# MLA prompt attention: the chunk mask as an extra matmul of one row, instead of a 97th row of queries and keys

## The reference, cut to what matters

```python
def _chunk_mask(q_pos, k_pos):
    return (k_pos // CHUNK)[None, :] <= (q_pos // CHUNK)[:, None]      # CHUNK = 64

def core(qb, qp):                                                      # qb: 128 queries
    s = jnp.einsum('bqhd,bkhd->bhqk', qb, k).astype(jnp.float32) * scale
    p = _masked_softmax(s, _chunk_mask(qp, kpos))
    return jnp.einsum('bhqk,bkhd->bqhd', p.astype(v.dtype), v)
```

## Time and profile before

| what | before |
|---|---|
| median of 3 runs | 4433.84 us (4428.59 to 4433.85) |
| the profiled execution | 4433.85 us |
| span of its trace | 4432.1 us |
| mean granted TensorE clock | 0.904 |
| MATMUL busy | 3834.7 us, 87% of the span |
| LDWEIGHTS busy | 3452.6 us, 78% |
| VectorE busy | 1939.3 us, 44% |
| ScalarE busy | 1147.2 us, 26% |
| GpSimd busy | 834.1 us, 19% |
| expanding stage, layers 0 and 1 | 704.5 to 716.3 us and 2870.6 to 2882.3 us |
| attention stage, layers 0 and 1 | 716.3 to 822 us and 2882.3 to 2988 us |

### The profile page before, as it was taken

How to read it: one execution, slowest core, us unless ns; L and a number is a source line. 1 busy time by engine, 2 the same in 40 slices (tenths; PEclk the granted TensorE clock), 3 DMA queues, 4 the chain that set the end, 5 groups by cost and what they waited for, 6 DMA issues and landing times. The chain is left out here.

```text
span 4432.1 us, 52290 instructions
## 1 busy us (share of the span) xinstructions
PE 3834.7 (87%) x21498; PEld 3452.6 (78%) x21498; DVE 1939.3 (44%) x3099; ACT 1147.2 (26%) x2101; POOL 834.1 (19%) x694
## 2 busy tenths in 40 slices
PE   3887798889779999999878769887988799999996
PEld 2865587579679999999866657864978799999995
DVE  3355243255334444454444634333542444444454
ACT  2244113333122221212133421242321321221211
POOL 1211011011122232222122100200112222232220
PEclk8999599789789999999989977995988899999998
DMA  4511121010101111111062210111001011111111
GB/s 150 165 59 55 44 70 70 22 48 1 31 27 39 43 43 39 39 39 43 19 181 92 72 61 30 61 57 67 1 6 44 28 39 39 43 39 38 44 39 47
DMA packets 102912, 229.80 MB, mean 52 GB/s; under 512 B 29156, under 2 KB 64484, under 8 KB 99016
## 3 DMA queue, kind: packets, MB, share of 16 engines
q1 hardware_dynamic: 102664, 226.36, 16.0%
HBM read 171.90 MB, written 52.07 MB: 51 GB/s over the span
## 5 line engine op out<-in xcount | busy, mean ns | idle before, releaser
L244 PE MATMUL PS<-h_split,w_split 128*128 128x384 f32 x3072 | 1069.1, 348 | 100.9 <-PEq L183 100.9
L246 PE MATMUL PS<-h_split,w_split 128*128 128x384 f32 x3072 | 1051.8, 342 | 0.0
L245 PE MATMUL PS<-h_split,w_split 128*128 128x384 f32 x3072 | 1048.6, 341 | 0.0
L239 POOL TENSOR_TENSOR w_split<-w_full,w_split 128x1024 fp32r<-128x1024 f32 (+1 forms) x196 | 494.4, 2523 | 1371.6 <-ACT w_split L231 1369.5
L244 PEld LDWEIGHTS PS<-h_split,w_split 128*128 128x128 f32 x3072 | 594.9, 194 | 116.7 <-issue 114.6
L245 PEld LDWEIGHTS PS<-h_split,w_split 128*128 128x128 f32 x3072 | 588.1, 191 | 1.4 <-issue 0.3
L246 PEld LDWEIGHTS PS<-h_split,w_split 128*128 128x128 f32 x3072 | 587.5, 191 | 0.0
L231 ACT CAST w_split<-w_full 128x1024 fp32r<-128x1024 f32 (+1 forms) x196 | 204.6, 1055 | 905.7 <-PE PS L246 763.5
L244 PE MATMUL PS<-ffn_act,w_split 128*128 128x384 f32 x1056 | 368.7, 349 | 71.8 <-DVE x L2035 54.5
L2035 DVE TENSOR_TENSOR x<-x,PS 128x384 f32<-128x384 f32 x528 | 287.1, 553 | 239.7 <-PE PS L246 239.5
L245 PE MATMUL PS<-ffn_act,w_split 128*128 128x384 f32 x1056 | 367.3, 348 | 0.0
(11 more groups left out here) (339 smaller groups left out, 5910.5 us busy)
## 6 DMA issues: line engine op xcount, KB each, us to landing
w_full<-in_w_up SPq DMA_DIRECT2D x88, 512.0 KB, 3.5
w_full<-in_w_down SPq DMA_DIRECT2D x44, 512.0 KB, 3.5
w_full<-in_w_in SPq DMA_DIRECT2D x40, 512.0 KB, 3.7
kq_keep<-split_rows SPq DMA_DIRECT2D x128, 128.0 KB, 2.4
kq_row<-kq_keep SPq DMA_DIRECT2D x32, 512.0 KB, 4.2
x_keep<-x SPq DMA_DIRECT2D x2, 4608.0 KB, 19.3
x<-x_keep SPq DMA_DIRECT2D x2, 4608.0 KB, 14.4
w_full<-in_w_out SPq DMA_DIRECT2D x16, 512.0 KB, 3.5
```

The source lines that it names most:

```text
L239: pool.tensor_tensor(ws[:, n % SSLOTS, 1, 0:w], wf[:, n % WSLOTS, 0:w], ws[:, n % SSLOTS, 0, 0:w].bitcast(F32), ALU.subtract).then_inc(w_l ...
L244: pe.matmul(out, w_hi, a_hi, start=first, stop=False)
L245: pe.matmul(out, w_hi, a_lo, start=False, stop=False)
L246: return pe.matmul(out, w_lo, a_hi, start=False, stop=last)
```

## The change

The mask no longer rides on a 97th row. GpSimd's four writes of row 96 are gone, and `qT` is declared with 96 rows. In `scores` the last 128 keys are no longer a matmul of their own, but part of the last piece of at most 512 keys; after it a matmul with one row, `first_half` (1 for the first 64 queries) times `second_half` (-1e30 for the last 64 keys), adds the mask to the last 128 columns in PSUM. Both operands are constants that already lie in row 0 of `cst8`. `prompt_attention` is called once, with `comps` 1 and `bias` None, so `masked` is true for the last piece of every unit.

```diff
-        qT = at("qT", [97, HEADS, TOK], R(30))
+        qT = at("qT", [96, HEADS, TOK], R(30))
...
                     for hh in range(HEADS):
                         pool.tensor_copy(kT[64:96, hh, :], krT[64:96, 0:SEQ])
-                    for half in range(2):
-                        cols = slice(64 * half, 64 * half + 64)
-                        pool.memset(qT[96:97, :, 0:SEQ].rearrange("p h (i c) -> p h i c", c=P)[:, :, :, cols],
-                                    1.0 - half)
-                        pool.memset(kT[96:97, :, :].rearrange("p h (i c) -> p h i c", c=P)[:, :, :, cols],
-                                    NEG * half)
...
-                    for at in range(0, n - P, 512):
-                        w = min(512, n - P - at)
-                        pe.matmul(S(v, 0)[:, at:at + w], q_of(hh, i, 96), k_of(hh, at, w, 96), start=True, stop=True)
-                    pe.matmul(S(v, 0)[:, n - P:n], q_of(hh, i, 97), k_of(hh, n - P, P, 97), start=True,
-                              stop=True).then_inc(s_ready, 1)
+                    for at in range(0, n, 512):
+                        w = min(512, n - at)
+                        masked = at + w == n and bias is None
+                        for c in range(comps):
+                            mm = pe.matmul(S(v, c)[:, at:at + w], q_of(hh, c, i), k_of(hh, c, at, w), start=True,
+                                           stop=not masked)
+                            if bias is None and at + w == n:
+                                mm = pe.matmul(S(v, c)[:, n - P:n], K8("first_half", 1), K8("second_half", 1),
+                                               start=False, stop=True)
+                            if at + w == n:
+                                mm.then_inc(s_ready, 1)
```

More of the change, by code:

```diff
@@ L2373, in _ @@
                     sp.wait_ge(y_moved, 32)
-                prompt_attention(block, sems, 1, lambda hh, i, r: qT[0:r, hh, i * P:(i + 1) * P],
-                                 lambda hh, at, w, r: kT[0:r, hh, at:at + w],
+                prompt_attention(block, sems, 1, lambda hh, c, i: qT[:, hh, i * P:(i + 1) * P],
+                                 lambda hh, c, at, w: kT[0:96, hh, at:at + w],
                                  lambda hh, t: val[:, t, hh * HD:(hh + 1) * HD], Pb, PTb, stat, None, o_mla)
```

## The result

The changed kernel takes 4475.38 us (median of 4 runs, 4470.8 to 4479.2) against 4433.54 us before: a ratio of 1.010, 95% interval 1.0084 to 1.0116. The direction was forecast, the size was not: +42 us instead of +19, outside the range of 4441 to 4461. The profiled execution took 4470.32 us, with a span of 4468.4 us.

The account below looks back on a forecast made before the run. Attention was taken as bound by a ring of waits of 4.80 us per unit through TensorE's scores. Masks cost 15.0 + 7.3 + 0.5 = 22.8 us, less 3.9 gained: +18.9, 4453 us, range 4441 to 4461.

Parts of the forecast that it names:

- The ring of waits: Attention units: turn, scores, VectorE's maxima and scaling wait in a circle of 4.80 us; TensorE work before `s_ready` lengthens every unit.
- mask hides in waits: Rival: scores are not in the ring of waits, so only the 3.9 us gain is left, 4430 us; chance 0.04.
- The join at 0: In `scores`, joining the last 128 keys to the piece before keeps the columns the same and saves 0 us.
- The count beside it: In `scores`, one matmul replaces two in blocks 1 to 3; the number doesn't fall for block 0 and from block 4 on.
- The pair at 0.22 us and not by its rows: The mask's two passes per unit, priced by columns: 0.22 us at full clock, 0.42 at half.
- The border at 0.10 us (0.14 at half clock): Change of shape from scores to mask, ahead of `s_ready`: that loss per unit, with ends of 0 and 0.20 us.
- The third rival, all loads exposed: Every weight load of the mask pair shows: 0.44 us a unit at full clock, 0.75 at half; 4461 us; chance 0.09.
- The number of units at half clock, 6 and 7: Attention units in layers 0 and 1 at half clock, the first two apart: 13, at 0.56 us each, 7.3 us.
- twice as long: Sign that the prediction is wrong: the attention's stretch at clock 0.5 doubles in length (or is gone).
- The gain of 3.9 us in the expanding stage: Removing GpSimd's writes ends the stage earlier: 1.10 us in layer 0 and 2.79 in layer 1.
- VectorE is late next: Expanding stage: without the writes VectorE ends it, 1.10 us before GpSimd's old end in layer 0, 2.79 in layer 1.
- The kept clock: Rival: a shorter idle gap keeps TensorE at 2.4 GHz when attention starts; +7.4 us, 4441 us; chance 0.07.

Follow-up runs that it names:

- nomask: Changed kernel without the mask matmul, so no masking and no writes of row 96: 4428.3 us, ratio 0.9997 to the kernel before.
- mask96: Changed kernel with the mask matmul over 96 rows of constants, the scores' shape, in place of one: 4447.4 us, ratio 1.0023 to the kernel before.
- mask_twice: Changed kernel with the one-row mask matmul issued twice in a row in each unit: 4493.2 us, ratio 1.0139 to the kernel before.
- cols64_1: Changed kernel with the one-row mask over only the last 64 keys of a unit: 4464.1 us, ratio 1.0063 to the kernel before.
- cols64_96: Changed kernel with the mask over 96 rows and only the last 64 keys: 4446.1 us, ratio 1.0026 to the kernel before.
- early1: Changed kernel with the one-row mask kept in blocks 0 to 2, 96 rows in the others: 4469.3 us, ratio 1.0086 to the kernel before.
- mask32: Changed kernel with the mask matmul over 32 rows in place of one: 4480.4 us, ratio 1.0102 to the kernel before.
- late1: Changed kernel with a 96-row mask in blocks 0 to 2, one row in blocks 3 to 7: 4451.7 us, ratio 1.0045 to the kernel before.
- border_only: Changed kernel with a 96-row mask, then a one-row matmul of 4 columns adding zeros: 4481.5 us, ratio 1.0117 to the kernel before.
- mask64: Changed kernel with the mask matmul over 64 rows in place of one: 4473.1 us, ratio 1.0087 to the kernel before.

## Why the prediction was wrong

**The ring of waits: right.** Each unit grew by what TensorE added ahead of `s_ready`; VectorE's and ScalarE's work and their order stayed as they were. The "mask hides in waits" rival is out: 44 us appeared in the two stages.

**The join at 0: right** (nomask, 4.79 for 4.80). The count beside it was not: a matmul falls away in blocks 5 to 7 too, which is how the records come to 96 fewer. At a price of 0 that changes nothing but the 2 us kept for the range. **The pair at 0.22 us and not by its rows: right**, by mask96 (0.21) and mask_twice (0.22). That a pass goes by its columns holds at 128 columns only: half of them save 0.05 us of a pair, not 0.11 (cols64_1, cols64_96). This much of the change alone is the 4447 us of mask96.

**The border at 0.10 us (0.14 at half clock): mis-sized, it is 0.20 (0.30).** The prediction read starts of records, from L1579 to L1618 0.10 late. But the first record behind a border begins together with its own weight load, so the second half of the loss lies inside the group and shows only at its end. The way back, L1618 to L1557, had it whole: 0.20. I had that as the upper end and took the lower. The third rival, all loads exposed, had a size near the measured one (0.44 per unit, 0.75 at half clock, against 0.41 and 0.72), but not its mechanism: loads within the pair are hidden (mask_twice).

**The number of units at half clock, 6 and 7: this is the step that failed.** The prediction took the overlap of the mask with the slow stretch from the trace before and let the stretch hold the units it had held there. It held 11 and 10 units apart from the first ones, 21 for the 13 of the sum, and in the units that fell into it `turn`, `scores` and `values` ran at half speed too. In its last part, "twice as long" was named as a sign of being wrong, but no term stood for it. This is the largest part of the miss, 14.9 of 23.7 us by the account below.

**The gain of 3.9 us in the expanding stage: 1.4.** "VectorE is late next" was right, its lateness read from one execution was not: it hangs on TensorE's clock in that stage. Where the clock was up through the stage (layer 0 of early1, L787 in 3.67 us) the stage took 8.91 us, 2.8 less than before, as was forecast for layer 1; where it came up late, 11.5.

**The kept clock: out.** The idle gap ahead of the attention did shrink, to 1.49 us in both layers, and the clock fell all the same, within 1 us of the stage's start in layer 0 and 4 us in layer 1.

The account, in the two traces, with 0.41 a unit at full clock and 0.72 at half: borders 47 x (0.41 - 0.32) + 13 x (0.72 - 0.56) = 6.3 us; expanding stage 2.5 us; what is left of the 44.0 us in the attention beyond 47 x 0.41 + 13 x 0.72 + 0.5 = 29.1, 14.9 us, is put down to the longer stretch. Together 23.7 us more than the 18.9 forecast: the 42.6 of the four stages. The medians differ by 41.8 us, the two profiled executions by 36.5, since stages that were not changed were faster in the second.

What stays open is why the clock comes back so late. Shown is that it follows the shape (mask96 against mask32), that it is decided in the first 12 units (early1 against late1), and that one-row matmuls with next to no columns are enough for most of it (border_only). Whether the columns of the small passes add to it is not shown: the traces say no (44 us with half the columns), all runs together say perhaps (+31 for +55). One reading fits most of this, that time in which TensorE is held up between passes delays the clock's return; that reading is argued, not shown by itself, and mask64 with 27 and 41 us shows how far one stage can differ from another with the same instructions.

## What to carry to other kernels

A matmul with fewer rows than its neighbours is not small: here its passes of 128 columns cost the same as full ones, and the change of shape on the path 0.20 us at 2.4 GHz and 0.30 at 1.2 (for 1, 32 and 64 rows; some 0.14 at 2.4 GHz where the weight columns were halved instead). Where a constant row or column can be padded to the neighbours' shape, padding cost nothing here; it gave back two thirds of the loss. Best of all was the row that rode along in a matmul that ran anyway.

Where a stage begins at half clock, small work with a change of shape that is added to TensorE there is to be priced twice: by itself, and by how much later the clock comes back for all that follows. The pair in the neighbours' shape had only the first price here (half-clock time of all runs -4 ± 13 us). A stretch at half clock seen in the trace before is a result of the work in it, not a given.

## What was not expected of the hardware

At half clock TensorE's records cover the stage almost wholly (39.94 of 40.90 us in layer 0) and yet the clock stayed at 1.2 GHz for some 40 us, while with the same work in one shape it came back after 11 to 16 us:

```profile
709.40:750.30 40.90, 39.94 (x119) 24.04 (x120) 11.05 (x38) 13.38 (x40) 0.00 (x0) 0.51 0.38 145
```

The busy time of the records does not tell how much TensorE worked: behind a border a pair that costs 0.42 us at half clock stands as a record group of 0.79 us, since its first record begins with its weight load.

Two passes of 4 columns in a strange shape cost nearly as much as two of 128 in that shape, within 0.1 us (border_only against the changed kernel, less the 96-row pair: 5.32 - 0.21 = 5.11 against 5.20).
